# Lagged follow-up steps, a separate gate ring and a spread-out recurrence in the first layer of a two-layer kernel

## The reference

```python
def _rglru_mixer(u, w_in, conv_w, conv_b, w_r, b_r, w_i, b_i, lam, w_out):
    proj = u @ w_in                                   # 2048 -> 4096
    xb, gate = proj[..., :2048], proj[..., 2048:]
    xc = causal_conv(xb, conv_w, 4 taps) + conv_b     # per channel, along the tokens
    xblk = xc.reshape(bn, s, 8, 256)
    r = sigmoid(einsum('bsnc,ncd->bsnd', xblk, w_r) + b_r)   # 8 blocks of 256 x 256
    i = sigmoid(einsum('bsnc,ncd->bsnd', xblk, w_i) + b_i)
    log_a = -8 * r * softplus(-lam)
    a = exp(log_a)
    bterm = sqrt(-expm1(2 * log_a)) * (i * xc)
    h = scan along the tokens: h[t] = a[t] * h[t-1] + bterm[t]
    y = h * silu(gate)
    return y @ w_out

h = x + rmsnorm(mixer(rmsnorm(x)));  h = h + sigmoid(h @ ple_w_gate) * (p @ ple_w_proj)
```

## Time and profile before

| | |
|---|---|
| median of 3 runs | 2128.64 us (2126.45 to 2130.31) |
| the profiled execution | 2130.43 us |
| its span from first to last instruction | 2128.6 us |
| PE, DVE, ACT busy in the span | 2070.1, 1559.6, 1026.7 us |
| mean granted TensorE clock | 0.991 |

### The profile page before, as it was taken

One profiled execution on the slowest core, in us unless ns is written; L12 is line 12 of the kernel. 1 busy time (PEld: TensorE's weight loads), 2 busy tenths in 40 slices (PEclk: granted clock), 3 DMA queues, 4 the chain that ended last, 5 costly groups with the idle time before them and its releaser, 6 DMA issues.

```text
span 2128.6 us, 31944 instructions
## 1 busy us (share of the span) xinstructions
PE 2070.1 (97%) x12888; PEld 1837.7 (86%) x12888; DVE 1559.6 (73%) x2326; ACT 1026.7 (48%) x1563; POOL 90.6 (4%) x73
## 2 busy tenths in 40 slices
PE   8888999999999999999999999999999999999997
PEld 8888999887888888899999888778888888888886
DVE  6677897868799776677788899576766766655655
ACT  6766444655622322545545455554444434434443
POOL 0000021020000000000000001300000000000012
PEclk9999999999999999999999999999999999999999
DMA  7556888567624566444346988645775765556552
GB/s 294 188 201 233 301 312 287 196 227 263 202 93 156 175 230 239 156 139 143 134 138 244 349 300 302 221 141 186 267 252 189 238 233 195 185 184 197 188 180 97
DMA packets 122548, 449.92 MB, mean 211 GB/s; under 512 B 13729, under 2 KB 13857, under 8 KB 121889
## 3 DMA queue, kind: packets, MB, share of 16 engines
q1 hardware_dynamic: 122400, 447.88, 61.6%
HBM read 443.63 MB, written 4.19 MB: 210 GB/s over the span
## 4 chain that ended last, share of the span: by engine, by line
PE 71%; DVE 2%; ACT 1%; issue 1%; POOL 0%; POOLq 0%; DVEq 0%; ACTq 0%
PE bank L841 70%; DVE WL L1524 0%; DVE AR L1531 0%; DVE SR L1531 0%; PE bank L973 0%; DVE AR L1524 0%; DVE AR L1624 0%; PE bank L1004 0%; ACT WH L1117 0%; ACT AR L1118 0%; POOL AR L2129 0%; ACT AR L1117 0%; ACT SR L1118 0%; POOL AR L2131 0%; ACT L1118 0%
## 5 line engine op out<-in xcount | busy, mean ns | idle before, releaser
L841 PE MATMUL bank<-SR,WH 128*128 128x512 f32 (+1 forms) x6880 | 1815.3, 352 | 33.9 <-DVE WL L1524 18.5
L841 PE MATMUL bank<-SR,WL 128*128 128x256 f32 (+1 forms) x5088 | 1211.6, 289 | 1.6 <-DVE SR L1531 1.6
L841 PEld LDWEIGHTS bank<-SR,WH 128*128 128x128 f32 x6880 | 1100.3, 191 | 94.0 <-DVE WL L1524 27.7
L841 PEld LDWEIGHTS bank<-SR,WL 128*128 128x128 f32 x5088 | 965.9, 190 | 157.1 <-DVE SR L1531 3.6
L1524 DVE TENSOR_TENSOR WL<-WF,WH 128x1024 fp32r<-128x1024 f32 x636 | 772.8, 1226 | 243.2 <-ACT WH L1117 242.8
L1117 ACT ACTIVATE WH<-WF 128x1024 fp32r<-128x1024 f32 x636 | 671.3, 1056 | 456.8 <-PE bank L841 420.7
L1117 ACT ACTIVATE AR<-bank 128x256 f32<-128x256 f32 (+1 forms) x264 | 105.1, 408 | 289.5 <-PE bank L841 275.6
L1531 DVE SCALAR_TENSOR_TENSOR AR<-WF,SM,AR 128x512 f32<-128x512 f32 (+1 forms) x210 | 209.2, 1022 | 4.5
L1524 DVE TENSOR_TENSOR AR<-AR 128x256 f32<-128x256 f32 (+9 forms) x374 | 154.3, 443 | 64.2 <-ACT AR L1118 41.3
L2124 POOL TENSOR_TENSOR AR<-AR 128x256 f32<-128x256 f32 x56 | 75.1, 1341 | 2020.9 <-ACT AR L1118 2020.6
L1524 DVE TENSOR_TENSOR AR<-AR,bank 128x256 f32<-128x256 f32 x112 | 47.2, 422 | 119.2 <-PE bank L841 91.2
(11 more groups left out here) (83 smaller groups left out, 436.7 us busy)
## 6 DMA issues: line engine op xcount, KB each, us to landing
WF<-in_mlp SPq DMA_DIRECT2D x256, 512.0 KB, 4.2
WF<-in_mod SPq DMA_DIRECT2D x192, 512.0 KB, 5.1
WF<-in_w_in SPq DMA_DIRECT2D x176, 512.0 KB, 4.2
WF<-in_a_in SPq DMA_DIRECT2D x64, 512.0 KB, 5.1
WF<-in_a_out SPq DMA_DIRECT2D x32, 512.0 KB, 6.0
WF<-in_ple_g SPq DMA_DIRECT2D x32, 512.0 KB, 4.7
WF<-in_w_out SPq DMA_DIRECT2D x32, 512.0 KB, 5.6
WF<-in_pw SPq DMA_DIRECT2D x16, 512.0 KB, 3.3
```

The lines of the kernel that those rows point to most:

```text
L841: return tensor.matmul(o, l, r, start=start, stop=stop, skip_group_check=True)
```

## The change

`AFTER` becomes 4 for `xb` and for `gate`. The conv step moves from `evac` to `after` 1, the taps to 2, the copy to 3, the subtraction to 4. For a gate tile the sigmoid moves to `after` 1, the products to 2, the copy to 3, the subtraction to 4. `GT` moves to memory of its own and has three slots for the tile and three for its sigmoid. `recurrence` has 27 parts instead of 16: ACT works in parts 3, 5, 7, 9 and makes the root in part 15 (before: 2, 3, 5, 7 and 10); DVE's inputs are in parts 8, 10, 12, 14 and its scans in 20, 22, 24, 26 (before: 4, 6, 8, 9 and 12 to 15).

```diff
-PARTS_OF = {"recurrence": 16, "prepare_ctx": 26, "conv_branch": 46, "conv_split": 8,
+PARTS_OF = {"recurrence": 27, "prepare_ctx": 26, "conv_branch": 46, "conv_split": 8,
...
-AFTER = {"xb": 3, "gate": 2, "pleg": 3, "cv": 1, "cg": 3, "ff": 1, "fb": 1, "q": 3, "gc": 1, "hout": 1, "gh": 4, "wout": 2, "mlp1": 2}
+AFTER = {"xb": 4, "gate": 4, "pleg": 3, "cv": 1, "cg": 3, "ff": 1, "fb": 1, "q": 3, "gc": 1, "hout": 1, "gh": 4, "wout": 2, "mlp1": 2}
...
-    H, GT, YS = area(16, 16), area(58, 4), split_area(32, 16)
+    H, GT, YS = area(16, 16), area(68, 6), split_area(32, 16)
...
-            if kind == "xb":
-                w.wait_ge(s_par, 32)
-                w.wait_ge(*left(what))
-                w.wait_ge(xc_lo, j - 7)
-                w.wait_ge(h_done, 4 * (j // 4 - 1))
-                act(XCf[:, j % 8, :], XB[:, j % 4, :], ACT.Identity, scale=par("conv_w", 48 + j), bias=par("conv_b", j)).then_inc(
-                    cv_a, 1)
-            elif kind == "gates":
+            if kind == "gates":
...
-            elif kind == "gate":
-                w.wait_ge(*left(what))
-                w.wait_ge(xc_v, 16)
-                w.wait_ge(ys_lo, j - 1)
-                act(GT[:, 2 + j % 2, :], GT[:, j % 2, :], ACT.Sigmoid).then_inc(ga, 1)
...
-            if kind == "xb" and n == 2:
+            if kind == "xb" and n == 1:
+                w.wait_ge(s_par, 32)
+                w.wait_ge(*left((kind, j)))
+                w.wait_ge(xc_lo, j - 7)
+                w.wait_ge(h_done, 4 * (j // 4 - 1))
+                act(XCf[:, j % 8, :], XB[:, j % 4, :], ACT.Identity, scale=par("conv_w", 48 + j), bias=par("conv_b", j)).then_inc(
+                    cv_a, 1)
+            elif kind == "xb" and n == 3:
                 w.wait_ge(xc_v, j + 1)
                 if j >= 8:
                     w.wait_ge(*full(("gates", (j // 4 - 2, 1, 1, 1))))
                 act(XCs[:, j % 8, 0, :], XCf[:, j % 8, :], ACT.Copy).then_inc(xc_hi, 1)
             elif kind == "gate" and n == 1:
+                w.wait_ge(*left((kind, j)))
+                w.wait_ge(gz, j - 2)
+                act(GT[:, 3 + j % 3, :], GT[:, j % 3, :], ACT.Sigmoid).then_inc(ga, 1)
+            elif kind == "gate" and n == 3:
                 w.wait_ge(gz, j + 1)
                 w.wait_ge(*full(("gates", (2 if j < 4 else 3, 1, 1, 1))))
-                act(YS[:, j, 0, :], GT[:, j % 2, :], ACT.Copy).then_inc(ys_hi, 1)
+                act(YS[:, j, 0, :], GT[:, j % 3, :], ACT.Copy).then_inc(ys_hi, 1)
...
         def recurrence(g):
-            yield
             for k in range(4):
+                yield
+                yield
                 ft = 4 * g + k
                 w.wait_ge(sp_ok, 1)
                 w.wait_ge(*left(("gates", (g, k // 2, 0, k % 2))))
...
                 act(RR[:, k, :], RR[:, k, :], ACT.Tanh, scale=psp[:, ft:ft + 1])
                 w.wait_ge(a_own, e)
                 act(T2[:, k, :], AA[:, k, :], ACT.Square).then_inc(dec, 1)
-                if k:
-                    yield
-                yield
-            yield
+            for _ in range(6):
+                yield
             w.wait_ge(rc_v, g + 1)
             act(T2, RR, ACT.Sqrt).then_inc(rc_s, 1)
-            for _ in range(7):
+            for _ in range(13):
...
-                w.wait_ge(cv_a, 16)
-                w.wait_ge(xc_v, 16)
-                w.wait_ge(ys_lo, j - 1)
-                tt(GT[:, j % 2, :], ps, RX, ALU.mult).then_inc(leave, 1)
+                w.wait_ge(x_sq, 2)
+                w.wait_ge(ys_lo, j - 2)
+                tt(GT[:, j % 3, :], ps, RX, ALU.mult).then_inc(leave, 1)
...
-            if kind == "xb" and n == 1:
+            if kind == "xb" and n == 2:
...
-            elif kind == "xb" and n == 3:
+            elif kind == "xb" and n == 4:
                 w.wait_ge(xc_hi, j + 1)
                 tt(XCs[:, j % 8, 1, :], XCf[:, j % 8, :], raw(XCs[:, j % 8, 0, :]), ALU.subtract).then_inc(xc_lo, 1)
-            elif kind == "gate" and n == 1:
-                w.wait_ge(ga, j + 1)
+            elif kind == "gate" and n == 2:
                 w.wait_ge(h_done, j + 1)
                 w.wait_ge(*left((kind, j)))
-                mark(tt(GT[:, j % 2, :], GT[:, j % 2, :], H[:, j, :], ALU.mult))
+                w.wait_ge(ga, j + 1)
+                mark(tt(GT[:, j % 3, :], GT[:, j % 3, :], H[:, j, :], ALU.mult))
                 marked()
-                tt(GT[:, j % 2, :], GT[:, j % 2, :], GT[:, 2 + j % 2, :], ALU.mult).then_inc(gz, 1)
-            elif kind == "gate":
+                tt(GT[:, j % 3, :], GT[:, j % 3, :], GT[:, 3 + j % 3, :], ALU.mult).then_inc(gz, 1)
+            elif kind == "gate" and n == 4:
                 w.wait_ge(ys_hi, j + 1)
-                tt(YS[:, j, 1, :], GT[:, j % 2, :], raw(YS[:, j, 0, :]), ALU.subtract).then_inc(ys_lo, 1)
+                tt(YS[:, j, 1, :], GT[:, j % 3, :], raw(YS[:, j, 0, :]), ALU.subtract).then_inc(ys_lo, 1)
...
-            yield
+            for _ in range(5):
+                yield
             for k in range(4):
-                if k:
-                    yield
-                    inputs(k - 1)
-                yield
-            inputs(3).then_inc(rc_v, 1)
-            yield
-            yield
-            yield
+                yield
+                yield
+                i = inputs(k)
+            i.then_inc(rc_v, 1)
+            for _ in range(6):
+                yield
             w.wait_ge(rc_v, g + 1)
             for k in range(4):
                 ft = 4 * g + k
...
                 vector.tensor_tensor_scan(H[:, ft, :], AA[:, k, :], II[:, k, :], 0.0, ALU.mult, ALU.add).then_inc(
                     h_done, 1)
                 yield
-            yield
+                yield
 
         def prepare_ctx(_):
             for q in range(4):
```

## The result

| | before | changed |
|---|---|---|
| median, both timed side by side | 2129.47 us (2126.45 to 2131.29, 4 runs) | 2104.66 us (2102.12 to 2106.07, 4 runs) |
| profiled execution | 2130.43 us | 2102.12 us |
| its span | 2128.6 us | 2100.3 us |

The ratio is 0.9883, 95% interval 0.9868 to 0.9898: 24.8 us faster by medians, where 24.0 was forecast.

A forecast was written before the change was run, and what follows sets the result against it. TensorE (PE), busy 2070.1 of 2128.6 us, bounds it, losing idle time and half-rate stretches. 25.6 us to win, less 0.7 for (d), less 0.9 for a half-rate piece: 24.0, so a median of 2104.6 us (2106.4 profiled); range 2099.5 to 2117.

The forecast's parts named there:

- the prize: PE's loss from 50 to 250 us: 25.6 us by idle time and clock, 28.1 by matmul count at 8.3 per us.
- 410 or more: Sign of being right: matmuls PE does per 50 us from 50 to 220 us, at clock 1.00.
- (a): Conv chain one block later: ends ScalarE's 6.36 us waits and the ping-pong; VectorE needs 4.7 us per tile against 5.8.
- (b): Recurrence laid out on PE's clock: a group costs PE 0 to 0.2 us of waits instead of 6.3.
- rival B: ScalarE stays late around gates, root 4 us later: 12 to 15 us gone, 2114 to 2117 us; chance 0.20.
- (c): Gate tiles' ring of three, later copy and subtraction: VectorE densest there, tightest low half 1.4 us left; nothing added.
- (d): Last gates stage: tile 15's subtraction now behind gate 1's evacuation and a low half; costs PE 0.7 us, at most 2.5.
- (e): Handover to the output product: pending steps flushed, four more instructions; costs nothing, at most 0.5 us.
- (f): Weight loads: SP's order unchanged, DMA share in the group goes from 0.57 to 0.68; costs nothing.
- The 0.9 us for a half-rate piece left: Taken off the sum for an even chance that one half-rate piece of some 3.5 us is left.
- D: Slower: ScalarE's conv step waits for the fourth scan; VectorE x late costs PE x - 1.1 per group; 2135; chance 0.07.
- C: No change: the prize is in the feed or given back at the handover; 2126 to 2130 us; chance 0.07.

The follow-up runs named there:

- the cube: The eight kernels with each of the change's three parts (X, G, S) in or out; ratios from 1 (none) to 0.9883 (all).
- gate_spread: Changed kernel with the conv chain back at its old places (gate steps and recurrence as changed); 2111.85 us.
- gate_only: Kernel before with only the gate tiles' ring and later gate steps added; 2123.32 us.
- spread_only: Kernel before with only the recurrence spread over 27 parts; 2120.0 us.
- conv_early: Changed kernel with only the conv step back at the tile's end; taps, copy and subtraction keep their later places; 2115.18 us.
- X: Part of the change: conv chain a step later; without the other two parts (ring of three kept) ratio 0.9928.
- G: Part of the change: the gate tiles' ring and their later steps; alone ratio 0.9971.
- lag_only: Changed kernel with the recurrence back in its old 16 parts; 2107.3 us.
- tables: Changed kernel with two one-column square roots added per recurrence on ScalarE, giving three more table loads per group; 2115.71 us.
- xb_lag_spread: Changed kernel with the gate tile's sigmoid, products, copy and subtraction at their old places, ring of three kept; 2111.49 us.
- late_scans: Changed kernel with the four scans four parts later, in parts 24, 26, 28, 30 of 31; 2113.25 us.
- S: Part of the change: the recurrence spread over 27 parts; alone ratio 0.9960.
- xb_lag: Kernel before with the conv chain's later steps and the ring; gate steps at old places, recurrence in 16 parts; 2111.93 us.

## Why the prediction was right

**What bounds it, and the prize.** Right. Idle time and clock gave 25.6 us as the whole prize, and 24.8 of it came. The count of matmuls gave 28.1, and 25.2 came by it; that count was set too high. The changed kernel does 406 and 405 matmuls in the first two stretches with only 0.31 and 0.48 us of idle time, so 8.3 per us isn't reached there even without waits, and the sign "410 or more" was missed in these two. The choice of the lower prize was right, though small waits, the reason given for it, are only 0.8 of the 2.9 us that the count has too many. The reading that both feeding engines had room and were in each other's way is shown by the busy times: ACT (1024 to 1028 us) and DVE (1558 to 1560 us) do the same work in all kernels of the cube, and the time goes from 2129 to 2105.

**(a) The conv chain.** Right, and it is the largest part: 15 us alone, 7 us on top of the other two (gate_spread to the change), and some 10 us for the conv step's place alone. With it the 6.36 us wait of the earlier trace rows is gone; without it a wait of 6.3 to 7.4 us is there whatever else is changed. What the text did not see is that there are two waits at that place. With the old recurrence it is the evacuation (before, gate_only), with the spread one the fourth scan (spread_only, gate_spread, conv_early). So the 7 and 10 us are mainly the price of the old place with late scans, and the 15 us that of the old place behind the evacuation; no run separates the two waits within one kernel.

**(b) The recurrence's layout.** From the table load on, the root's end was laid out 18.5 us later and came 19.2 later; the fourth scan's end 29.2 and came 29.6; the period was laid out at 31.3 to 31.8 and is 31.9. The conv step tied to the fourth scan ends before its cast can start, as laid out. From the scan's end to the cast's start were laid out 1.1 us and came 1.2, but the layout forgot the conv step itself, 0.6 us, so the margin is 0.5. The sigmoid that was to free its bank 0.2 us early is 0.17 us late. So every place was right to within 0.7 us, and the margins to 0.6 us. That the spread is worth little once X and G are there (3 us, lag_only to the change, which is within the intervals of the two; the mod pair in gate tile 15 moves by the same 3.0) was not worked out in the prediction, which took the parts as one.

**The table load.** By the page "ScalarE: Activation LUTs", section "What ACT_TABLE_LOAD costs", of the Trainium skill, a drain of 1.38 us goes with each switch. The loads of the changed kernel and of tables are 1.28 us with the next instruction 0.01 to 0.02 us behind, also back to back with a one-column root between them. The trace does not agree with the page here, and the sum by 1.28 was the right one. The run with three more loads shows what the page's figure would have meant: 4.1 us more of ACT a group took 11 us of the gain, where rival B of the prediction had said 2114 to 2117 and 2115.71 was measured.

**(c) The gate ring.** The step had "I add nothing": right for the changed kernel, which has no wait there. But the text put all of the worth into (a) and (b). Without the later gate steps, the ring kept, the kernel is 7 us slower (xb_lag_spread), and ring and steps alone win 6: the copy of a gate tile kept ACT standing for DVE from 145 us on (21.1 us in seven waits, instead of 1.7 in one) as the conv step did before it. That is within the whole prize, so the sum isn't touched, but its parts were.

**(d) The added wait.** Forecast 0.7 us of PE for the last subtraction. That is there, as the weight load's wait of 0.33 us for DVE SR at 149.33. Half of the size; another 0.35 us at 147.86, for the evacuation of gate 1 that now stands ahead of it, was not foreseen, and together they are the 0.7. By place it is a little more: from the mod pair ahead of gates 3 to the next one are 13.68 us (141.23 to 154.91), in gate_spread, which has the subtraction at its old place, 12.70 (152.02 to 164.72). So the later conv chain costs 1.0 us at the last gates stage, and the best kernel there is the one without it. The subtraction ended at 149.28, 29.5 us behind the first matmul after gates 2 (119.74), laid out at 29.4; PE came to it later than the 28.7 laid out.

**(e), (f).** Gate 15's last block runs 2.93 us behind its mod pair, which puts a_out's first matmul at 244.6 where near 247 was laid out (this execution won 26.8 us up to there, not 24.4), and PE has no wait between 150 and 250 us; DMA's share is 0.67 to 0.69 in the groups, where 0.68 was worked out. Nothing, as said.

**The 0.9 us for a half-rate piece left.** None was left in the first layer of the profiled execution. With 0.7 for (d) that makes the sum 24.9 by the prize of 25.6, against 24.8 measured by idle time and clock. The 24.8 us by medians has an interval of 3 us either way, so that it is the same to the tenth is luck.

**The rivals.** B and D did not happen, but both exist: tables shows B's price, late_scans D's mechanism. D's threshold was right in kind: with the conv step 3.4 us late PE waits 2.20 and 1.68 us in two groups, 1.2 to 1.7 us less, where the text had x - 1.1. C is out: the DMA share rose with PE and no weight's DMA held PE; two casts waited 2.7 and 2.1 us for theirs.

One thing stays open. PE's half-rate pieces before 45 us differ between executions: of the twelve profiles five have none behind 5 us, the others one or two, and X, G or S doesn't tell them apart (lag_only has none, xb_lag, with the same conv chain, has two, at 13.9 and 37.8). The changed kernel, late_scans and tables, which differ only in the recurrence behind gates 0, have none, one and two there. The same stretch, in xb_lag:

```profile
13.90:17.30 3.40, 3.40 (x19) 3.40 (x18) 2.75 (x4) 2.07 (x4) 0.00 (x0) 0.50 1.03 411
```

and in lag_only:

```profile
13.90:17.30 3.40, 3.04 (x26) 2.84 (x25) 2.60 (x4) 2.23 (x4) 0.00 (x0) 1.00 1.03 412
```

What decides it wasn't found. A piece of 3.4 us is up to 1.7 us lost, so two move a single profile by up to 3.4 us (an estimate from these lengths), and the gains are taken from medians.

## What to carry to other kernels

When two helper engines each have room but wait for each other inside one tile, move the reader of each handed-over value one step later than its writer, all along the chain, and give the buffers one more slot: that took off most of the loss, and the work didn't change. It can cost a little where a result is read soon, as at the last gates stage here (1.0 us). Count the worth of such parts by place in the program, not in sum: where one part has already made PE run nearly full, the next one can add little. Alone X and S are worth 15 and 9 us, together 18; G is worth nothing ahead of gates 3 and most of the gain behind it. Then check where the recurrence or any long in-order run sits by moving it both ways: here earlier was free, four parts later cost 8.6 us.

## What the runs showed that I had not expected

Half-rate stretches stand behind surprisingly short idle times. In the profiles of before and of the ten runs there are 17 idle times of PE of 2.2 to 2.9 us between 45 and 245 us. 14 of them have a stretch at 1.2 GHz, 3.4 or 6.8 us long, beginning within 2 us of the idle time's end or inside it; three (2.28, 2.54, 2.55 us) have none. Idle times of 0.8 to 1.97 us that stood alone had none behind them. Two pairs of shorter ones in the profile of before, 1.71 and 0.82 us, and 1.84 and 1.18 us seven microseconds apart, had a stretch too, 6.8 and 3.4 us long; in gate_spread a pair of 0.81 and 1.32 us had none. So a wait of 2.2 us and more was in most cases paid for once more: 3.4 us at half rate are up to another 1.7 us.
